# Issuing the first weight unit's three transfers from ScalarE's queue in a two-layer hybrid decoder trunk

## What is computed

```python
mem_n = _rmsnorm(mem, mem_norm_g)
for i in range(DEPTH):                      # DEPTH = 2
    j = i // N_MIXERS
    h = _rmsnorm(x, mix_norm_g[i])
    mix = _ssd_mix(h, mem_n, ssd_w_in[j], ...) if i % 2 == 0 else _sb_mix(h, mem_n, sb_w_in[j], ...)
    x = x + mix
    x = x + _swiglu(_rmsnorm(x, ffn_norm_g[i]), ffn_w_gate_up[i], ffn_w_down[i])
return x
```

## Time and profile before

| | us |
|---|---|
| median of 3 runs | 796.65 (796.47 to 797.05) |
| the profiled execution | 797.15 |
| its span in the trace | 795.2 |
| TensorE busy | 790.5 |
| VectorE busy | 619.1 |
| ScalarE busy | 434.7 |
| GpSimd busy | 65.9 |

### The profile page before, as it was taken

How to read it: one execution, slowest core, us unless ns; L and a number is a source line. 1 busy time by engine, 2 the same in 40 slices (tenths; PEclk the granted TensorE clock), 3 DMA queues, 4 the chain that set the end, 5 groups by cost and what they waited for, 6 DMA issues and landing times.

```text
span 795.2 us, 9708 instructions
## 1 busy us (share of the span) xinstructions
PE 790.5 (99%) x3728; PEld 657.3 (83%) x3728; DVE 619.1 (78%) x940; ACT 434.7 (55%) x516; POOL 65.9 (8%) x94
## 2 busy tenths in 40 slices
PE   9999999999999999999999999999999999999998
PEld 5988888888888888888888888888888888888886
DVE  4698899887758788888978878768667778888862
ACT  5677774476437354454337676666653735445430
POOL 4010032310000000000000000114330000000000
PEclk9999999999999999999999999999999999999999
DMA  7854456533546665665546545443445566565551
GB/s 247 291 165 158 159 199 218 193 132 121 183 144 196 205 199 176 207 196 177 209 159 211 171 148 168 149 159 108 156 156 162 166 205 194 182 208 193 180 209 53
DMA packets 85453, 141.38 MB, mean 178 GB/s; under 512 B 3438, under 2 KB 50960, under 8 KB 85408
## 3 DMA queue, kind: packets, MB, share of 16 engines
q1 hardware_dynamic: 84416, 139.73, 52.7%
q10 hardware_dynamic: 608, 0.93, 0.3%
q0 software_dynamic: 384, 0.11, 0.1%
HBM read 139.68 MB, written 1.07 MB: 177 GB/s over the span
## 4 chain that ended last, share of the span: by engine, by line
PE 99%; DMA 0%; DVE 0%; DVEq 0%; issue 0%
PE acc L1378 29%; PE acc L1380 29%; PE acc L1379 29%; PE bank L1375 4%; PE acc L1600 1%; PE bank L1500 1%; PE bank L1545 1%; PE bank L1528 1%; PE bank L1573 1%; PE bank L1551 1%; PE bank L1563 1%; DMA xr<-in_x 0%; PE bank L1574 0%; PE bank L1552 0%; PE bank L1510 0%; PE bank L1506 0%
## 5 line engine op out<-in xcount | busy, mean ns | idle before, releaser
L1026 DVE TENSOR_TENSOR lo<-raw,hi 128x2048 fp32r<-128x2048 f32 (+2 forms) x129 | 291.5, 2266 | 62.1 <-ACT hi L695 60.9
L695 ACT ACTIVATE hi<-raw 128x2048 fp32r<-128x2048 f32 (+2 forms) x129 | 241.4, 1880 | 83.4 <-DMA raw<-in_ffn_w_gate_up 41.6
L1378 PE MATMUL acc<-lo,aT_hi 128*128 128x512 f32 (+1 forms) x660 | 257.6, 390 | 0.0
L1380 PE MATMUL acc<-hi,aT_lo 128*128 128x512 f32 (+1 forms) x660 | 253.9, 385 | 0.0
L1379 PE MATMUL acc<-hi,aT_hi 128*128 128x512 f32 (+1 forms) x660 | 253.5, 384 | 0.0
L1380 PEld LDWEIGHTS acc<-hi,aT_lo 128*128 128x128 f32 x660 | 123.9, 188 | 25.1
L1379 PEld LDWEIGHTS acc<-hi,aT_hi 128*128 128x128 f32 x660 | 124.0, 188 | 24.1 <-issue 0.2
L1378 PEld LDWEIGHTS acc<-lo,aT_hi 128*128 128x128 f32 x660 | 124.0, 188 | 24.1 <-issue 0.2
L1245 DVE STREAM_TRANSPOSE uT<-un 32x256 f32<-32x256 f32 (+1 forms) x192 | 79.4, 414 | 3.1
L1378 PE MATMUL acc<-lo,uT_hi 128*128 128x512 f32 x176 | 68.6, 390 | 0.0
L1380 PE MATMUL acc<-hi,uT_lo 128*128 128x512 f32 x176 | 68.5, 389 | 0.0
(11 more groups left out here) (217 smaller groups left out, 863.8 us busy)
## 6 DMA issues: line engine op xcount, KB each, us to landing
raw<-in_ffn_w_gate_up SPq DMA_DIRECT2D x88, 512.0 KB, 4.5
raw<-in_ffn_w_down SPq DMA_DIRECT2D x22, 1024.0 KB, 4.7
raw<-in_sb_w_in SPq DMA_DIRECT2D x20, 1024.0 KB, 4.9
raw<-in_ssd_w_in SPq DMA_DIRECT2D x14, 1024.0 KB, 5.1
raw<-in_mem_w_kv SPq DMA_DIRECT2D x8, 1024.0 KB, 5.0
raw<-in_ssd_w_out SPq DMA_DIRECT2D x8, 1024.0 KB, 4.8
raw<-in_sb_w_out SPq DMA_DIRECT2D x8, 1024.0 KB, 4.7
seg<-cs_rows SPq DMA_DIRECT2D x6, 384.0 KB, 5.1
```

What stands on the lines that cost most here:

```text
L695: return nc.scalar.activation(out_, in_, func, **k)
L1026: v.tensor_tensor(lo[w % RING][:, c], raw[w % RING][:, c], hi[w % RING][:, c].bitcast(F), ALU.subtract).then_inc(lo_ready, 1)
L1378: mm(ps, stat_hi, mov_lo, start=first, stop=False)
L1380: return mm(ps, stat_lo, mov_hi, start=False, stop=last)
```

## The change

The function `first_in` moves from SyncE's program to ScalarE's. ScalarE issues w0, w1 and w2 after the gains and ahead of the table load; SyncE issues only the quarters of x and everything from unit 1 on. Sizes, semaphores, destinations and all waits of the compute engines are as they were.

```diff
@@ SyncE's program
-            def first_in(i):
-                src, n = SRC[0]
-                kk = slice(*FIRST[i])
-                dst = raw[0][:, 0:n].rearrange("p (t n) -> p t n", t=UNIT_KT)
-                sem = S(f"first_landed{i}") if i else raw_landed[0]
-                sp.dma_start(dst[:, kk, :], src[:, kk, :]).then_inc(sem, 16)
-
             x_in(0, 0)
-            first_in(0)
             x_in(1, 0)
-            first_in(1)
-            first_in(2)
             for t in range(TOK):
                 x_in(t, 1)
                 piece_in(1, t)
@@ ScalarE's program
             act.dma_start(vrow[0:16, 2, :], mix_norm_g.rearrange("l (f p) -> (l f) p", p=P)).then_inc(S("gain_landed"), 16)
+
+            def first_in(i):
+                src, n = SRC[0]
+                kk = slice(*FIRST[i])
+                dst = raw[0][:, 0:n].rearrange("p (t n) -> p t n", t=UNIT_KT)
+                sem = S(f"first_landed{i}") if i else raw_landed[0]
+                act.dma_start(dst[:, kk, :], src[:, kk, :]).then_inc(sem, 16)
+
+            for i in range(len(FIRST)):
+                first_in(i)
             act.preload_act_table_set("natural_log_exp_and_others")
```

## The result

| | before | changed |
|---|---|---|
| median of 21 runs, us | 796.86 (796.07 to 798.52) | 798.53 (796.70 to 799.97) |
| profiled execution, us | 797.15 | 797.44 |
| its span, us | 795.2 | 795.7 |

The ratio is 1.0017, with a 95% interval of 1.001 to 1.0023: 0.17% slower. It weighs all the runs; the two medians alone are 0.21% apart. So the change lies right at the 0.2% that the prediction called "same", under it by the ratio and just over it by the medians, and 21 runs of each set it apart from no change. The 21 times of the changed kernel are not one cloud. Eight lie from 796.70 to 797.44 and thirteen from 798.30 to 799.97; of before, one of 21 lies above 798. The median of the lower eight is 797.08, only 0.2 above that of before, so nearly all of the loss is in the upper group. The trace at hand is of the lower one and shows little of it.

What follows compares the result with a forecast made beforehand. The prediction took TensorE as the bound, busy 790.5 of 795.2 us. Issues and table load cost 0, sharing 0.5 with x00's 0.1 inside it: 796.65 + 0.5 = 797.15, rounded to 797.1 us; range 796.0 to 798.7.

Steps and rivals of the forecast that it cites:

- same: Whole kernel: a time within about 0.2%, 1.6 us, of no change; given chance 0.86.
- rival 2: Start of TensorE: late x00 or a hole ahead of (0, 0) prolongs half-rate passes; +1.9 to +2.6 us, chance 0.13.
- What bounds the kernel, and that only the first microseconds move: Whole span: TensorE is busy 790.5 of 795.2 us; everything after about 15 us is the same program.
- Issue times and table load: SyncE and ScalarE start: w1, w2 issued 0.5 us earlier; table load from about 2.6 to 3.9 us, cost 0.
- Sharing by halves: Two queues at the start: equal shares make w1 and w2 late; 0 to 1.05 us, taken as 0.5.
- the forecast's main term: Holes ahead of products using w1 and w2, from sharing the paths: 0 to 1.05 us, taken as 0.5.
- w0, "0 to 0.2": Product (0, 0): w0 lands with x10 at 5.6 us instead of 4.95; 0 to 0.2 us, inside the other terms.
- x00, "0 to 0.3, I take 0.1": First transfer: w0 running beside x00 delays its landing 0 to 0.3 us, taken as 0.1 within the w2 hole.
- the reading that x00 would wait for the other queue's writes: DMA rule at the start: x00 and w1 wait for the other queue's writes; sum at the upper end, about 1.05 us.

Runs made afterwards that it cites:

- before again: The kernel before, unchanged, profiled a second time; its trace is the second trace of before: 796.93 us median, ratio 1.0002.
- seven products of ones: The kernel before with seven products of ones at the start instead of five: 796.98 us median, ratio 1.0003.
- The fill with ones: The changed kernel with four products of ones instead of one between the transposes of x00 and product (0, 0): 797.16 us median, ratio 1.0003.
- The single-queue run: The kernel before with one swap, SyncE issuing x00, x10, w0, w1, w2: 798.88 us median, ratio 1.0018.

## Why the prediction was right, and where it was not

The time, 798.53, is inside the range of 796.0 to 798.7, near its upper end, and by the ratio the change is "same within 0.2%", narrowly. The forecast of 797.15 is 1.4 us short of it: instead of +0.5 the medians of 21 runs each moved +1.7. That both still hold is in good part luck: the forecast rested on late w1 and w2, and the loss came from a late w0 and the low level after it. That is rival 2, which the range took in only by its lower part.

- *What bounds the kernel, and that only the first microseconds move*: right. From the first product of split weights to the end of the span every trace has the same length: 795.2 - 17.83 = 777.4 before, 795.7 - 18.23 = 777.5 changed, 796.6 - 19.27 = 777.3 in the upper group, 794.7 - 17.23 = 777.5 before again.
- *Issue times and table load*: right. The load starts at 2.69 and ends at 3.97; ScalarE's first activation is still released by VectorE. Nothing was paid for it.
- *Sharing by halves*: right in kind. w1 was forecast at 7.7 to 8.4 and landed at 7.8, w2 at 10.0 to 11.4 and landed at 10.7. w1's hole is 0.09 us, no more than at the same place in the second trace of before (0.08), and no wait of TensorE names it; w2's is 0.35. So of the forecast's main term only w2's part exists, and in the lower group only; in the trace of the upper group TensorE is so late that w2 is there before it.
- *w0, "0 to 0.2"*: this is the step that failed. I took w0's landing as 5.6 and the need as 5.86. It landed at 6.17 to 6.29, and the need was about 5.1. Both numbers came from one trace that is unlike the later ones on both counts. Its x10 landed at 5.6, where the kernel before has 6.45 in its second trace and 6.70 with seven products of ones; its x00 landed at 4.27, where they have 3.4. The method was sound: laid on the second trace, equal shares put w0 with x10 at 6.45, w1 halfway between 7.1 and 8.5, at 7.8, and w2 with p10 at 10.5, each within 0.3 us of what was measured. The two errors, 0.6 and 0.8 us, less the 0.26 us between 5.6 and 5.86, and the 0.14 us from landing to first pass are the hole of 1.2 us.
- *x00, "0 to 0.3, I take 0.1"*: nothing. With w0 issued 0.44 us behind it, x00 takes 2.6 to 2.8 us, with w0 in the other queue or in its own (3.5 in the trace of before, where one queue held both); the reading that x00 would wait for the other queue's writes is not borne out. Issued with it, w0 goes with an x00 that is 1.4 us later.
- *Rival 2, a longer slow start, chance 0.13*: this is what happened in 21 of the 32 runs of the changed kernel. Its place and its condition ("a hole opens ahead of (0, 0)") were right, and its total came out: +1.9 to +2.6 forecast, and the middle of the upper group, 798.97, lies 2.1 above the median of before. The terms of that total were not right. Between the second traces of the two kernels, (0, 0) starts 1.4 us later and (0, 1) 2.1 us later, so the delay of the start counts 1.4 where the prediction had holes of 0.3 to 1.0, and the level the rest where it had 1.6, with two passes (three in the upper traces of two other kernels here) and four transposes slow. The 0.34 us for a slow pass was too small as well, as the two passes at 1.58 were a mixture of both levels; a slow pass costs 0.42 to 0.47 more. The chance was far too low. My argument against it, that the runs before lie close together, only told that the level change is steady while TensorE has no hole; it says nothing for a kernel that opens one. The fill with ones shows the cause: same late w0, no hole, no upper group.

The Trainium skill's rule that the DMA engines alternate between queues with work ("DMA: Bandwidth & Descriptors", "Queues, rings and completion order") agrees with all three pieces: laid on the second trace of before, equal shares put w0, w1 and w2 at 6.45, 7.8 and 10.5 us, and they landed at 6.17, 7.8 and 10.7. The single-queue run shows that for w0 the order of bytes alone does the same.

Left open: which executions with the hole fall in which group. The landings of w0 in the two traces differ by 0.12 us only, and no run here separates what decides it. A wait alone doesn't: behind x10's waits of 0.8 and 1.8 us, in the runs with w0 back on SyncE's queue and with x10 held back, the eight passes took 3.63 us, all at the high level. Also open is why in the one trace of before x00 and the gains landed 0.8 us later, w0, w1 and w2 0.4 to 0.6 us later, and x10 0.8 us earlier than in the second.

No version here beats the kernel before. Its order of issue, x00, w0, x10, w1, w2 on one queue, is the order of need.

## What to carry to other kernels

At a start where the paths are full, count for a transfer's landing the bytes ahead of it and beside it before you count the time of its issue: here w1 was issued 0.5 us earlier and landed at 7.8 us instead of 7.1 to 7.6. Keep transfers in the order of need and don't let one that is needed later run beside one that is needed next; no split over two queues that was tried here did better than one queue. Price a wait of TensorE at its start as the hole and then the passes that run at the low level after it; here the low level behind a 1.2 us hole cost about 1 us more between two traces, and products of ones in the hole took it back. Take landings and slack from more than one trace: here one trace had x00 0.8 us later and x10 0.8 us earlier than the next, which made w0's new landing look early enough and the need for it look late. And look at the single run times before the median, since two groups tell of a second mechanism.

## What the runs showed of the hardware

- An 8 KB transfer issued behind a 256 KB one on the same queue took 4.0 to 4.5 us to land; issued first it took 2.2 to 2.3 (3.1 in the trace of before).
- Two 256 KB transfers issued in the same moment from two queues took 4.0 and 4.2 us to land in one trace, 4.4 and 4.6 in another; the first one took 2.6 to 2.8 with the next one 0.44 us behind it (3.5 in the trace of before).
- TensorE's level after a hole of 1.2 us differed between executions of one program whose landings agreed within 0.12 us: two passes in 1.10 or in 2.04 us, while the granted clock column read 1.00 in both.
- With two queues at work, three transfers landed at 6.17, 7.8 and 10.7 us, within 0.3 us of where equal shares put them on the landings of one queue.
